# Two of four sums of weight tiles made by adding transfers; turned signs; the head's tokens in pairs of tiles

## The chip, the cores and the metric

The kernel runs on one core of one Trainium2 chip. The metric is the device time of one execution in microseconds; lower is better. TensorE multiplies matrices, VectorE and ScalarE work on tiles element by element, GpSimd does small vector work and can issue transfers, and SyncE (SP) issues nearly all loads. A transfer moves data between the chip's memory and SBUF through 16 DMA engines shared by all queues.

## The reference, cut to what matters

One decoder layer, float32, 256 tokens of 2048 features: a half-step SwiGLU, a mixer (latent attention and a gated recurrence), cross-attention to 256 memory tokens, and a second half-step SwiGLU. The change touches the two SwiGLUs (FFN 1 and 2), which hold most of the products:

```python
def swiglu(h, w_gate, w_up, w_down):          # w_gate, w_up: 2048 x 5504; w_down: 5504 x 2048
    return (jax.nn.silu(h @ w_gate) * (h @ w_up)) @ w_down

h = rmsnorm(x, ffn1_norm[l])
x = x + 0.5 * swiglu(h, ffn1_w_gate[l], ffn1_w_up[l], ffn1_w_down[l])
...
h = rmsnorm(x, ffn2_norm[l])
x = x + 0.5 * swiglu(h, ffn2_w_gate[l], ffn2_w_up[l], ffn2_w_down[l])
```

## The kernel before

Every float32 product is made as three matmuls in a faster float format: each operand is split into a high part (ScalarE, `w_hi`, `hT_hi`) and the rest (VectorE, `w_lo`, `hT_lo`), and TensorE does hi·hi, lo·hi and hi·lo. A tile is 128 x 512 weights (256 KB); the tokens are two tiles of 128.

Weights stream through a ring `raw` of RAW = 6 slots of four tiles (1 MB). SP fills slot c (semaphore `raw_loaded`, one for each place in the ring), ScalarE makes `w_hi` (a ring of three), VectorE `w_lo` (in place of the raw weights), TensorE uses it and counts `slot_used` twice for a slot. SP may load slot c when slot c - 6 is used up. All engines run their own instruction list in written order and meet only at semaphores, so nothing reorders itself.

Both FFNs begin with one plain pair of blocks (gate and up, four slots each). The head is that pair in FFN 1: slots 0 to 3 also need the turned tokens `xT` (16 tiles, tile k by semaphore `xT_in`), which ScalarE and VectorE split (`x_turned`). Everything after it is done in 28 "duos": pairs of 512-wide blocks, gate and up for the up-projections, two neighbouring column blocks for the down-projection. Two duos, the last up-pair of each FFN, are 384 wide. In a duo, three units (four in the first half's down-projections) each cover two tiles of depth in both blocks of weights with the seven products of a Strassen-Winograd scheme in place of eight, and plain slots cover the rest. A unit takes two slots: `raws[n]` holds its four weight tiles, the slot after it the four sums of them that the seven products need. VectorE made these sums (`combine`, L1249, L1251, L1253), after which ScalarE (`hi_made`, L798) and VectorE (`lo_parts`, L1261) split them. A duo of three units runs in TensorE as unit, plain, unit, plain, unit, plain (first block), then three plain slots (second block). A unit is 21 matmuls: `small` (P1), `acc` (A12), for the first unit of a duo then `tr` (P7), `small` (P6), `acc`, `acc`, `acc`; for later units one product of the raw slot comes before P7. P7 and P6 are the first that read the made slot.

`combine` before the change:

```python
dve.wait_ge(loaded[c % RAW], landed(c))
dve.wait_ge(slot_used, 2 * (c + 1 - RAW + 1))
v.tensor_tensor(made[:, 0:2, :], b[:, 1:4:2, :], b[:, 0:2, :], ALU.subtract).then_inc(ev("combined"), 1)
dve.wait_ge(ev("combined"), 2 * n + 1)
done(v.tensor_tensor(made[:, 2, :], b[:, 3, :], made[:, 0, :], ALU.subtract))
done.wait()
v.tensor_tensor(made[:, 3, :], b[:, 2, :], made[:, 2, :], ALU.subtract).then_inc(ev("combined"), 1)
```

Of the kernel before, what the change touches and what calls it, by code (L numbers as in the profile page):

```python
# [20 lines left out]
ALU = mybir.AluOpType  # L21
# [3 lines left out]
P = 128  # L25
NW = 512
# [101 lines left out]
def layer(nc, a, out):  # L128
# [18 lines left out]
    with ctx:  # L147
# [121 lines left out]
        loaded = [sem(f"raw_loaded{s}") for s in range(RAW)]  # L269
        hi_done = sem("hi_done")  # L270
# [10 lines left out]
        xT_in = [sem(f"xT_in{k}") for k in range(4 + 3)]  # L281
# [113 lines left out]
        for duo in DUOS:  # L395
            for r in duo.raws:
                fetches[r], fetches[r + 1] = 2 if duo.up else 1, 0
        M = slots["mix"]

        def landed(c):  # L400

            return 16 * sum(fetches[c % RAW:c + 1:RAW])

# [57 lines left out]

        @block.sync
        def _(sp):
# [6 lines left out]

            def rows_of(w, k0, tiles, cols):
                return w[k0 * P:(k0 + tiles) * P, cols].rearrange("(k p) n -> p k n", p=P)

            def load_duos(f):

                wg, wu, wd = (a[f"ffn{f}_w_{n}"][0] for n in ("gate", "up", "down"))
                for m in range(FIRST[f], LAST[f] + 1):
# [3 lines left out]
                    def load_unit(c, k):  # L481
# [43 lines left out]
            def load_first():  # L525
# [69 lines left out]
        def _(pool):  # L595
# [47 lines left out]
            done.wait()  # L643
            norm("x1")
            norm("mem")
# [40 lines left out]
            norm("x4")  # L686


        @block.scalar
        def _(act):  # L690
# [3 lines left out]
            def hi(c, rep, tiles, width):  # L694

                c += rep
                for i, (k0, k1) in enumerate(halves(tiles)):
                    if c == 1 and i == 0:
# [184 lines left out]
            def first_slots(s):  # L883

                for k in range(4):
# [5 lines left out]
                    else:  # L891
                        act.wait_ge(xT_in[3 + s], 16)
                        x_turned(4 * s + k)
                if s == 0:
                    act.wait_ge(first_hi, 4)
                    act.sem_inc(hi_done, 2)
                else:
                    hi(s, 0, 4, NW)
# [281 lines left out]
        def _(dve):  # L1180
# [4 lines left out]
            def lo(c, rep, tiles, width):  # L1185

                c += rep
                for i, (k0, k1) in enumerate(halves(tiles)):
                    dve.wait_ge(hi_done, 2 * c + i + 1)
# [38 lines left out]
            def token_sums(s1, rest, src):  # L1228

                done(v.tensor_tensor(s1, src[:, 0, P:SEQ], src[:, 1, P:SEQ], ALU.add))  # L1230
# [4 lines left out]
                v.tensor_tensor(rest[2], src[:, 1, 0:P], rest[0], ALU.subtract).then_inc(ev("sums_made"), 1)  # L1235
# [8 lines left out]
            def combine(c, n, width):  # L1244
# [63 lines left out]
            def take_parts(m):  # L1308
# [1095 lines left out]
```

## Time and profile before

| | |
|---|---|
| median of 3 runs | 1889.87 us (1889.83 to 1889.91) |
| profiled execution, its own time | 1891.52 us |
| its span, first to last instruction | 1889.6 us |
| PE busy | 1877.6 us, 99% |
| PEld (weight loads, beside PE) | 1576.3 us, 83% |
| VectorE (DVE) busy | 1550.7 us, 82% |
| ScalarE (ACT) busy | 1077.2 us, 57% |
| GpSimd (POOL) busy | 96.6 us, 5% |
| DMA | 362.55 MB, 57% of the 16 engines' time |
| granted TensorE clock | 1.00 throughout |

Busy time is the union of an engine's instructions; a matmul's modelled duration (0.39 us for 512 columns) overlaps the next one's. The busy share of an engine is an average over stages; what an engine waited for, and where, is read in the waits and the timeline.

### The profile page before, as it was taken

To read this page: it belongs to the slowest core of one execution; us is meant where nothing else is said; L and a number is where in the kernel's file an instruction comes from. 1 tells how busy PE (TensorE), PEld (TensorE's weight loads), DVE (VectorE), ACT (ScalarE), POOL (GpSimd) and SP (SyncE) were. 2 spreads that over 40 slices of the span, in tenths; PEclk is the share of its full clock that TensorE was granted. 3 is DMA by queue.
4 is the path that set the end of the run, shared out by engine and by line. 5 is a ranking of instruction groups with operands and counts; after the bars stand their busy time and mean duration, and the time that the engine had idled before them with its cause. 6 is when DMAs were issued, how large, how long until landed. Compare 5 with 4: busy or idle time off the path is not lost.

```text
span 1889.6 us, 23072 instructions
## 1 busy us (share of the span) xinstructions
PE 1877.6 (99%) x8836; PEld 1576.3 (83%) x8836; DVE 1550.7 (82%) x1955; ACT 1077.2 (57%) x1437; POOL 96.6 (5%) x98
## 2 busy tenths in 40 slices
PE   8999999999999999999999999999999999999999
PEld 7888888888889888988888888888888888888987
DVE  6999998888999877655666774689999978899986
ACT  6665555546556547545475655566565554555553
POOL 0000000000000001312250000000000000000000
PEclk9999999999999999999999999999999999999999
DMA  9655565655556674555443654456656665655654
GB/s 328 231 182 192 200 207 200 223 188 195 196 174 209 219 237 154 170 170 179 141 156 105 207 181 153 156 178 200 200 179 203 220 216 174 212 190 185 199 191 171
DMA packets 176862, 362.55 MB, mean 192 GB/s; under 512 B 8048, under 2 KB 19312, under 8 KB 176112
## 3 DMA queue, kind: packets, MB, share of 16 engines
q1 hardware_dynamic: 176464, 360.89, 57.2%
q8 instruction: 70, 1.15, 0.2%
q14 instruction: 40, 0.33, 0.1%
q10 hardware_dynamic: 288, 0.19, 0.0%
HBM read 358.95 MB, written 2.10 MB: 191 GB/s over the span
## 4 chain that ended last, share of the span: by engine, by line
PE 96%; DVE 1%; ACT 1%; DMA 1%; POOL 1%; issue 0%; SPq 0%; DVEq 0%; ACTq 0%; POOLq 0%
PE acc L1889 19%; PE acc L1887 19%; PE acc L1888 19%; PE acc L1876 8%; PE acc L1878 8%; PE acc L1877 8%; PE small L1887 2%; PE small L1889 2%; PE small L1888 2%; PE small L2088 2%; PE tr L1845 1%; PE tr L1889 1%; PE tr L1887 1%; PE tr L1888 1%; PE tr L1903 1%; DMA w_raw<-in_ffn_w_gate 0%
## 5 line engine op out<-in xcount | busy, mean ns | idle before, releaser
L1261 DVE TENSOR_TENSOR w_lo<-w_raw,w_hi 128x1024 fp32r<-128x1024 f32 (+2 forms) x720 | 724.7, 1060 | 66.3 <-ACT w_hi L704 46.7
L704 ACT ACTIVATE w_hi<-w_raw 128x1024 fp32r<-128x1024 f32 (+4 forms) x552 | 513.2, 963 | 167.3 <-PE acc L1889 123.3
L1887 PE MATMUL acc<-w_hi,hT_hi 128*128 128x512 f32 (+1 forms) x920 | 354.9, 386 | 0.0
L1889 PE MATMUL acc<-w_lo,hT_hi 128*128 128x512 f32 (+1 forms) x920 | 353.3, 384 | 0.0
L1888 PE MATMUL acc<-w_hi,hT_lo 128*128 128x512 f32 (+1 forms) x920 | 352.9, 384 | 0.0
L1190 DVE TENSOR_TENSOR w_lo<-w_raw,w_hi 128x1024 fp32r<-128x1024 f32 (+1 forms) x184 | 217.9, 1225 | 60.2 <-ACT w_hi L704 58.8
L798 ACT ACTIVATE w_hi<-w_raw 128x1024 fp32r<-128x1024 f32 (+1 forms) x176 | 182.3, 1044 | 114.0 <-DVE w_raw L1249 59.8
L1887 PE MATMUL acc<-w_hi,actT_hi 128*128 128x512 f32 x548 | 213.9, 390 | 0.0
L1889 PE MATMUL acc<-w_lo,actT_hi 128*128 128x512 f32 x548 | 213.3, 389 | 0.0
L1888 PE MATMUL acc<-w_hi,actT_lo 128*128 128x512 f32 x548 | 213.2, 389 | 0.0
L1889 PEld LDWEIGHTS acc<-w_lo,hT_hi 128*128 128x128 f32 x920 | 172.7, 188 | 32.7
L1887 PEld LDWEIGHTS acc<-w_hi,hT_hi 128*128 128x128 f32 x920 | 172.7, 188 | 32.2 <-DVE stage L1318 0.2
L1888 PEld LDWEIGHTS acc<-w_hi,hT_lo 128*128 128x128 f32 x920 | 172.8, 188 | 31.8
L791 ACT ACTIVATE w_hi<-w_raw 128x512 fp32r<-128x512 f32 (+3 forms) x176 | 142.7, 829 | 94.4 <-PE acc L1889 93.5
L1876 PE MATMUL acc<-w_hi,hT_hi 128*128 128x512 f32 (+1 forms) x480 | 186.7, 389 | 4.5 <-DVE w_lo L1190 3.7
L1878 PE MATMUL acc<-w_lo,hT_hi 128*128 128x512 f32 (+1 forms) x480 | 184.5, 384 | 0.0
L1877 PE MATMUL acc<-w_hi,hT_lo 128*128 128x512 f32 (+1 forms) x480 | 184.2, 384 | 0.0
L1889 PEld LDWEIGHTS acc<-w_lo,actT_hi 128*128 128x128 f32 x548 | 102.9, 188 | 21.5
L1888 PEld LDWEIGHTS acc<-w_hi,actT_lo 128*128 128x128 f32 x548 | 102.9, 188 | 21.3
L1887 PEld LDWEIGHTS acc<-w_hi,actT_hi 128*128 128x128 f32 x548 | 102.9, 188 | 21.2
L1876 PEld LDWEIGHTS acc<-w_hi,hT_hi 128*128 128x128 f32 x480 | 90.2, 188 | 22.2 <-issue 4.5
L1249 DVE TENSOR_TENSOR w_raw<-w_raw 128x1024 f32<-128x1024 f32 (+1 forms) x88 | 105.4, 1198 | 0.0
(306 smaller groups left out, 2547.9 us busy)
## 6 DMA issues: line engine op xcount, KB each, us to landing
w_raw<-in_ffn_w_down SPq DMA_DIRECT2D x68, 1024.0 KB, 5.2
w_raw<-in_w_in SPq DMA_DIRECT2D x36, 1024.0 KB, 5.0
w_raw<-in_ffn_w_gate SPq DMA_DIRECT2D x38, 768.0 KB, 4.3
w_raw<-in_ffn_w_up SPq DMA_DIRECT2D x38, 768.0 KB, 4.4
w_raw<-in_ffn_w_gate SPq DMA_DIRECT2D x56, 512.0 KB, 3.9
w_raw<-in_ffn_w_up SPq DMA_DIRECT2D x54, 512.0 KB, 4.8
w_raw<-in_ffn_w_up SPq DMA_DIRECT2D x26, 1024.0 KB, 5.9
w_raw<-in_ffn_w_gate SPq DMA_DIRECT2D x24, 1024.0 KB, 5.1
```

What stands on the lines that cost most here:

```text
L704: nc.scalar.activation(piece(w_hi, c % SPLIT, k0, k1, width), piece(raw, c % RAW, k0, k1, width), ACT.Copy).then_inc(hi_done, 1)
L791: nc.scalar.activation(piece(w_hi, c % SPLIT, k0, k1, width), piece(raw, c % RAW, k0, k1, width), ACT.Copy).then_inc(hi_done, 1)
L798: nc.scalar.activation(piece(w_hi, c % SPLIT, k0, k1, width), piece(raw, c % RAW, k0, k1, width), ACT.Copy).then_inc(hi_done, 1)
L1190: v.tensor_tensor(piece(w_lo, c % RAW, k0, k1, width), piece(raw, c % RAW, k0, k1, width), piece(w_hi, c % SPLIT, k0, k1, width).bitcast(F ...
L1249: v.tensor_tensor(made[:, 0:2, :], b[:, 1:4:2, :], b[:, 0:2, :], ALU.subtract).then_inc(ev("combined"), 1)
L1261: v.tensor_tensor(piece(w_lo, c % RAW, k0, k1, width), piece(raw, c % RAW, k0, k1, width), piece(w_hi, c % SPLIT, k0, k1, width).bitcast(F ...
L1876: mm(dst, xh, wh, start=first and kk == 0, stop=False)
L1877: mm(dst, xl, wh, start=False, stop=False)
L1878: ins = mm(dst, xh, wl, start=False, stop=last and kk == tiles - 1)
L1887: mm(dst, lhs_hi, wh, start=first, stop=False)
L1888: mm(dst, lhs_lo, wh, start=False, stop=False)
L1889: return mm(dst, lhs_hi, wl, start=False, stop=last)
```

## The change

It does four things.

1. SP loads, right behind the first slot of a unit, two tiles of the right block (`right_rows`) into the first half of the made slot. GpSimd, once these have landed, issues two transfers that add in flight: the unit's first left tile onto the first of them, and the first right tile onto the second (`add_weights`, semaphore `weights_added`).
2. VectorE's `combine` waits for these and makes only the other two sums, by one-tile additions.
3. The scheme's signs are turned to suit, since transfers can add and not subtract: in the sums of activations (`token_sums`) and in two of the additions of `take_parts`.
4. In the head, token tiles 4 to 15 come in six transfers of two tiles in place of three of four; SP's waits in between are on other semaphores; ScalarE and VectorE split two token tiles, then half a weight slot, in turn, and TensorE waits for token tiles two at a time (`later_piece`).

```diff
+        def summed(c):
+            return 32 * sum(e == c or e < c and e % RAW == c % RAW for d in DUOS for e in [r + 1 for r in d.raws])
...
                             sp.dma_start(dst, rows_of(wd, f0 + k, 2, slice(2 * d.block * NW, 2 * (d.block + 1) * NW))).then_inc(loaded[c % RAW], 16)
+                        sp.wait_ge(slot_used, 2 * (c + 1 - RAW + 1))
+                        made = raw[:, (c + 1) % RAW, :].rearrange("p (k n) -> p k n", k=4)
+                        sp.dma_start(made[:, 0:2, 0:d.width], right_rows(m, k, 2)).then_inc(loaded[(c + 1) % RAW], 16)
...
-                x_tiles(4, 4, xT_in[4])
+                x_tiles(4, 2, xT_in[4])
                 sp.wait_ge(first_in[1], 16)
                 for b, done in enumerate((first_in[4], loaded[1])):
+                    if b:
+                        x_tiles(6, 2, xT_in[5])
...
-                for s in range(2, 4):
-                    sp.wait_ge(xT_in[2 + s], 16)
-                    x_tiles(4 * s, 4, xT_in[3 + s])
+                for s, landed_ in ((2, first_in[3]), (3, loaded[1])):
+                    sp.wait_ge(landed_, 16)
+                    x_tiles(4 * s, 2, xT_in[2 + 2 * s])
                     load(s, 0, rows_of(wg, 4 * s, 4, slice(0, NW)), 4, NW)
+                    x_tiles(4 * s + 2, 2, xT_in[3 + 2 * s])
...
+            def add_weights(f):
+                for m in range(FIRST[f], LAST[f] + 1):
+                    d = DUOS[m]
+                    for n, c in enumerate(d.raws):
+                        c += 1
+                        made = raw[:, c % RAW, :].rearrange("p (k n) -> p k n", k=4)
+                        pool.wait_ge(loaded[c % RAW], landed(c))
+                        for i, rows in enumerate((left_rows, right_rows)):
+                            nc.gpsimd.dma_start(made[:, i:i + 1, 0:d.width], rows(m, d.units[n], 1), accum_op=ALU.add).then_inc(added[c % RAW], 16)
+
             norm("x1")
+            add_weights(1)
             norm("mem")
...
             norm("x4")
+            add_weights(2)
...
                 for i, (k0, k1) in enumerate(MADE_PARTS):
-                    act.wait_ge(ev("combined"), 2 * n + i + 1)
+                    if i == 0:
+                        act.wait_ge(added[c % RAW], summed(c))
+                    else:
+                        act.wait_ge(ev("combined"), 2 * n + 2)
...
-                done(v.tensor_tensor(s1, src[:, 0, P:SEQ], src[:, 1, P:SEQ], ALU.add))
+                done(v.tensor_tensor(s1, src[:, 0, P:SEQ], src[:, 1, P:SEQ], ALU.subtract))
...
-                v.tensor_tensor(rest[2], src[:, 1, 0:P], rest[0], ALU.subtract).then_inc(ev("sums_made"), 1)
+                v.tensor_tensor(rest[2], src[:, 1, 0:P], rest[0], ALU.add).then_inc(ev("sums_made"), 1)
...
                 dve.wait_ge(loaded[c % RAW], landed(c))
-                dve.wait_ge(slot_used, 2 * (c + 1 - RAW + 1))
-                v.tensor_tensor(made[:, 0:2, :], b[:, 1:4:2, :], b[:, 0:2, :], ALU.subtract).then_inc(ev("combined"), 1)
+                dve.wait_ge(added[(c + 1) % RAW], summed(c + 1))
+                v.tensor_tensor(made[:, 2, :], made[:, 1, :], b[:, 0, :], ALU.add).then_inc(ev("combined"), 1)
                 dve.wait_ge(ev("combined"), 2 * n + 1)
-                done(v.tensor_tensor(made[:, 2, :], b[:, 3, :], made[:, 0, :], ALU.subtract))
-                done.wait()
-                v.tensor_tensor(made[:, 3, :], b[:, 2, :], made[:, 2, :], ALU.subtract).then_inc(ev("combined"), 1)
+                v.tensor_tensor(made[:, 3, :], made[:, 2, :], b[:, 2, :], ALU.add).then_inc(ev("combined"), 1)
...
-                done(v.tensor_tensor(nat[:, 0, 0:w], p5, nat[:, 0, 0:w], ALU.add))
+                done(v.tensor_tensor(nat[:, 0, 0:w], p5, nat[:, 0, 0:w], ALU.subtract))
                 done.wait()
-                v.tensor_tensor(nat[:, 1, 0:w], p5, gate[:, 1, 0:w], ALU.add).then_inc(ev("parts_taken"), 1)
+                v.tensor_tensor(nat[:, 1, 0:w], p5, gate[:, 1, 0:w], ALU.subtract).then_inc(ev("parts_taken"), 1)
```

VectorE's list at the second unit of the first duo, before; L1249, L1251 and L1253 are the sums, L1261 low parts of weights, L1270 that of activations:

```order
42 L1249 TENSOR_TENSOR w_raw<-w_raw 128x1024 [waits slot_used,raw_loaded5]
43 L1251 TENSOR_TENSOR w_raw<-w_raw 128x512 [waits combined]
44 L1253 TENSOR_TENSOR w_raw<-w_raw 128x512 [waits dve_done]
45 L1261 TENSOR_TENSOR w_lo<-w_raw,w_hi 128x512 [waits hi_done]
46 L1261 TENSOR_TENSOR w_lo<-w_raw,w_hi 128x1024 [waits hi_done,combined]
47 L1270 TENSOR_TENSOR actT_lo<-tr,actT_hi 128x512 [waits turn_hi]
```

The same place in the changed kernel (its L1300 and L1302 are the sums, L1310 and L1319 the low parts):

```order
47 L1300 TENSOR_TENSOR w_raw<-w_raw 128x512 [waits weights_added0,raw_loaded5]
48 L1302 TENSOR_TENSOR w_raw<-w_raw 128x512 [waits combined]
49 L1310 TENSOR_TENSOR w_lo<-w_raw,w_hi 128x512 [waits hi_done]
50 L1310 TENSOR_TENSOR w_lo<-w_raw,w_hi 128x1024 [waits hi_done,combined]
51 L1319 TENSOR_TENSOR actT_lo<-tr,actT_hi 128x512 [waits turn_hi]
```

The two-tile sum is gone, and the first instruction left waits for the adding transfers with everything else behind it.

GpSimd's list in the changed kernel after the norm of the first tokens (before, the norm of the memory stood here next):

```order
8 L632 TENSOR_SCALAR rsq<-sums 128x2 [waits sums_x1,pool_done]
9 L634 TENSOR_TENSOR rsq<-rsq,minus_half 128x2 [waits pool_done]
10 L683 DMA w_raw<-in_ffn_w_gate 128x512 [waits raw_loaded3]
11 L683 DMA w_raw<-in_ffn_w_up 128x512
12 L683 DMA w_raw<-in_ffn_w_gate 128x512 [waits raw_loaded0]
```

Two adding transfers for each unit follow on each other in the order of the units.

SP's list in the head, before; `xT_raw` are the turned tokens:

```order
8 L528 DMA xT_raw<-in_x_turned 128x1024
9 L538 DMA w_raw<-in_ffn_w_gate 128x2x512 [waits first_slot_in1]
10 L538 DMA w_raw<-in_ffn_w_gate 128x2x512
11 L528 DMA xT_raw<-in_x_turned 128x1024 [waits xT_in4]
12 L469 DMA w_raw<-in_ffn_w_gate 128x4x512
13 L528 DMA xT_raw<-in_x_turned 128x1024 [waits xT_in5]
14 L469 DMA w_raw<-in_ffn_w_gate 128x4x512
```

And in the changed kernel:

```order
8 L555 DMA xT_raw<-in_x_turned 128x512
9 L567 DMA w_raw<-in_ffn_w_gate 128x2x512 [waits first_slot_in1]
10 L555 DMA xT_raw<-in_x_turned 128x512
11 L567 DMA w_raw<-in_ffn_w_gate 128x2x512
12 L555 DMA xT_raw<-in_x_turned 128x512 [waits first_slot_in3]
13 L495 DMA w_raw<-in_ffn_w_gate 128x4x512
14 L555 DMA xT_raw<-in_x_turned 128x512
15 L555 DMA xT_raw<-in_x_turned 128x512 [waits raw_loaded1]
16 L495 DMA w_raw<-in_ffn_w_gate 128x4x512
17 L555 DMA xT_raw<-in_x_turned 128x512
```

The tokens stand in smaller pieces around the weights, and SP waits for weights that land earlier, no longer for the tokens themselves.

## Rows read from the trace of the kernel before

**Rows 1.** The page: span, busy time and share of the two busiest engines.
```profile
span 1889.6 us, 23072 instructions
...
PE 1877.6 (99%) x8836; PEld 1576.3 (83%) x8836; DVE 1550.7 (82%) x1955; ACT 1077.2 (57%) x1437; POOL 96.6 (5%) x98
```

**Rows 2.** Waits of PE: total us, times, longest.
```profile
PE acc L1876 <- DVE w_lo L1190: 3.7, 2, 1.9
```

**Rows 3.** Timeline of PE, head: start, us, engine, what [idle before].
```profile
14.14 0.47 PE L1876 MATMUL acc<-w_hi,hT_hi 128*128 128x512 f32 x1 [1.78 <-DVE w_lo L1190]
...
21.80 0.47 PE L1876 MATMUL acc<-w_hi,hT_hi 128*128 128x512 f32 x1 [1.94 <-DVE w_lo L1190]
```

**Rows 4.** Timeline of PE, first unit of the third duo.
```profile
140.32 0.39 PE L1888 MATMUL acc<-w_hi,hT_lo 128*128 128x512 f32 x1
140.55 0.39 PE L1889 MATMUL acc<-w_lo,hT_hi 128*128 128x512 f32 x1
141.44 0.50 PE L1887 MATMUL tr<-w_hi,hS_hi 128*128 128x512 f32 x1 [0.50 <-DVE w_lo L1261]
...
142.58 0.50 PE L1887 MATMUL small<-w_hi,hS_hi 128*128 128x512 f32 x1 [0.17 <-DVE w_lo L1261]
```

**Rows 5.** One line's instructions: ns min/median/max, first and last start.
```profile
L1249 DVE TENSOR_TENSOR w_raw<-w_raw x88: 946/1216/1221, 49.4 to 1848.5; 128x1024 f32<-128x1024 f32 x82, 128x768 f32<-128x768 f32 x6
```

**Rows 6.** Windows: busy time (count) of each engine, clock, DMA share, GB/s.
```profile
core 0: us, PE busy (x) PEld busy (x) DVE busy (x) ACT busy (x) POOL busy (x), PEclk, DMA share, GB/s
...
16.00:19.00 3.00, 3.00 (x15) 2.47 (x14) 1.68 (x4) 1.71 (x4) 0.00 (x0) 1.00 0.55 148
...
30.00:45.00 15.00, 15.00 (x67) 12.40 (x67) 7.79 (x17) 10.88 (x16) 0.34 (x2) 1.00 1.01 381
...
145.00:300.00 155.00, 155.00 (x700) 128.10 (x699) 148.13 (x178) 89.09 (x110) 0.00 (x0) 1.00 0.61 205
```

**Rows 7.** Units' first products (P1) in three duos: durations, first and last start.
```profile
L1887 PE MATMUL small<-w_hi,hT_hi x3: 389/389/389, 183.2 to 203.2; 128*128 128x512 f32 x3
...
L1887 PE MATMUL small<-w_hi,hT_hi x3: 389/389/389, 394.2 to 413.3; 128*128 128x512 f32 x3
...
L1887 PE MATMUL small<-w_hi,hT_hi x3: 333/334/334, 563.0 to 578.5; 128*128 128x384 f32 x3
```

**Rows 8.** Timeline of SP: second half of the third unit's load.
```profile
187.88 0.47 SPq L487 DMA_DIRECT2D w_raw<-in_ffn_w_up  x1
```

**Rows 9.** The page's DMA issues: count, KB each, median us to landing.
```profile
w_raw<-in_ffn_w_down SPq DMA_DIRECT2D x68, 1024.0 KB, 5.2
...
w_raw<-in_ffn_w_gate SPq DMA_DIRECT2D x56, 512.0 KB, 3.9
```

**Rows 10.** DMA issues at 187.88, and at 33.09.
```profile
w_raw<-in_ffn_w_up SPq DMA_DIRECT2D x1, 512.0 KB, 4.9
...
w_raw<-in_ffn_w_up SPq DMA_DIRECT2D x1, 512.0 KB, 11.0
```

**Rows 11.** Timeline of DVE before the third unit of the fourth duo.
```profile
199.18 1.21 DVE L1249 TENSOR_TENSOR w_raw<-w_raw 128x1024 f32<-128x1024 f32 x1
...
201.76 5.22 DVE L1261 TENSOR_TENSOR w_lo<-w_raw,w_hi 128x512 fp32r<-128x512 f32 x5
```

**Rows 12.** Timeline of ACT, head: tokens, then high parts of slot 1.
```profile
10.08 1.71 ACT L901 ACTIVATE hT_hi<-xT_raw,gains 128x256 fp32r<-128x256 f32 x4 [0.64 <-DMA xT_raw<-in_x_turned]
11.70 2.03 ACT L704 ACTIVATE w_hi<-w_raw 128x1024 fp32r<-128x1024 f32 x2
```

**Rows 13.** The chain that ended last, head: start, us, what.
```profile
10.46 8.86 DMA w_raw<-in_ffn_w_gate
```

**Rows 14.** Timeline, the first unit of all: sums, low part, first product.
```profile
49.37 1.22 DVE L1249 TENSOR_TENSOR w_raw<-w_raw 128x1024 f32<-128x1024 f32 x1
...
51.95 4.09 DVE L1261 TENSOR_TENSOR w_lo<-w_raw,w_hi 128x512 fp32r<-128x512 f32 x4
...
54.52 0.39 PE L1887 MATMUL small<-w_hi,hT_hi 128*128 128x512 f32 x1
```

More of the change, by code:

```diff
@@ L269, in layer @@
         loaded = [sem(f"raw_loaded{s}") for s in range(RAW)]
+        added = [sem(f"weights_added{s}") for s in range(RAW)]
         hi_done = sem("hi_done")
@@ L280, in layer @@
         gains_in, ident_in, const_in, x_in, mem_in = sem("gains_in"), sem("ident_in"), sem("const_in"), sem("x_in"), sem("mem_in")
-        xT_in = [sem(f"xT_in{k}") for k in range(4 + 3)]
+        xT_in = [sem(f"xT_in{k}") for k in range(4 + 6)]
         first_in = [sem(f"first_slot_in{k}") for k in range(4 + 1)]
@@ L396, in layer @@
             for r in duo.raws:
-                fetches[r], fetches[r + 1] = 2 if duo.up else 1, 0
+                fetches[r], fetches[r + 1] = 2 if duo.up else 1, 1
         M = slots["mix"]
@@ L459, in layer, with rows_of, columns_of, right_rows @@
         block = ctx.enter_context(nc.Block())
+        def rows_of(w, k0, tiles, cols):
+            return w[k0 * P:(k0 + tiles) * P, cols].rearrange("(k p) n -> p k n", p=P)
+        def columns_of(m, side):
+            d = DUOS[m]
+            f0 = HALVES[d.half][0]
+            n0 = (f0 + 4 * d.block) * P if d.up else (2 * d.block + side) * NW
+            w = a[f"ffn{d.f}_w_{('gate', 'up')[side] if d.up else 'down'}"][0]
+            return w, 0 if d.up else f0, slice(n0, n0 + d.width)
+        def right_rows(m, k, tiles):
+            w, k0, cols_ = columns_of(m, 1)
+            return rows_of(w, k0 + k, tiles, cols_)
+        def left_rows(m, k, tiles):
+            w, k0, cols_ = columns_of(m, 0)
+            return rows_of(w, k0 + k, tiles, cols_)
         @block.sync
@@ L469, in load @@
                 sp.dma_start(dst, src).then_inc(loaded[c % RAW], 16)
-            def rows_of(w, k0, tiles, cols):
-                return w[k0 * P:(k0 + tiles) * P, cols].rearrange("(k p) n -> p k n", p=P)
             def load_duos(f):
@@ L692, in _, with hi @@
             flat_stage = stage[:].rearrange("p a b -> p (a b)")
-            def hi(c, rep, tiles, width):
+            def hi(c, rep, tiles, width, part=None):
                 c += rep
                 for i, (k0, k1) in enumerate(halves(tiles)):
+                    if part not in (None, i):
+                        continue
                     if c == 1 and i == 0:
@@ L891, in first_slots @@
                     else:
-                        act.wait_ge(xT_in[3 + s], 16)
+                        if k % 2 == 0:
+                            act.wait_ge(xT_in[2 + 2 * s + k // 2], 16)
                         x_turned(4 * s + k)
+                        if k % 2:
+                            hi(s, 0, 4, NW, part=k // 2)
                 if s == 0:
@@ L896, in first_slots @@
                     act.sem_inc(hi_done, 2)
-                else:
-                    hi(s, 0, 4, NW)
             def x_turned(k):
@@ L1183, in _, with lo @@
             flat_stage = stage[:].rearrange("p a b -> p (a b)")
-            def lo(c, rep, tiles, width):
+            def lo(c, rep, tiles, width, part=None):
                 c += rep
                 for i, (k0, k1) in enumerate(halves(tiles)):
+                    if part not in (None, i):
+                        continue
                     dve.wait_ge(hi_done, 2 * c + i + 1)
@@ L1414, in first_slots @@
                                         w_hi[:, 0, k * NW:(k + 1) * NW].bitcast(F32), ALU.subtract).then_inc(first_lo, 1)
+                    elif k % 2:
+                        lo(s, 0, 4, NW, part=k // 2)
                 if s == 0:
@@ L1417, in first_slots @@
                     dve.sem_inc(lo_done, 2)
-                else:
-                    lo(s, 0, 4, NW)
             def x_turned(k):
@@ L1854, in of, with later_piece, wait @@
                 return lambda m, t: src[:, t, col0 + m * P:col0 + (m + 1) * P]
+            def later_piece(s):
+                def wait(kk):
+                    if kk % 2 == 0:
+                        pe.wait_ge(x_lo, 4 * s + kk + 2)
+                return wait
             def first_piece(kk):
@@ L2050, in first_pair @@
                         if f == 1 and b == 0:
-                            pe.wait_ge(x_lo, 4 * s + 1 if s == 0 else 4 * s + 4)
-                            pieces = first_piece if s == 0 else None
+                            pieces = first_piece if s == 0 else later_piece(s)
                         slot(c + 4 * b + s, 0, B0 + b, hT_hi, hT_lo, 4 * s, 4, NW, s == 0, s == 3, pieces=pieces)
```

1 line of the change is left out of this document (added).

## The prediction, made blind

> **What bounds the kernel now.** Read the page first: TensorE has matmuls in flight for 1877.6 of 1889.6 us, VectorE works 82% of the span [rows 1]. The waits of PE say how little TensorE gives away: 3.7 us for w_lo at L1190, and nothing else of size inside the two FFNs [rows 2]. The timeline shows where: idle for 1.78 us before 14.14 and 1.94 us before 21.80 [rows 3]. Between these places a 128x512 matmul starts every 0.23 us (140.32 to 140.55) [rows 4]. The one loss inside an FFN stands in the same rows: the first unit of the third duo starts its third product (three matmuls) at 141.44, 0.89 us after the matmul before in place of 0.23, and the fourth at 142.58, 1.14 us later in place of 0.69. That is 0.66 + 0.45 = 1.1 us, some 1.2 with the restart behind it. So VectorE is busy but almost nowhere late, and the instructions taken from it can give back only what is idle: 3.7 us in the head and 1.2 us here. Everything else the change does can only cost.
>
> **What VectorE loses.** Before, a unit's sums are a subtraction of two tiles, 1.2 us, 88 times [rows 5], and two of one tile; from 199.18 to 201.76 the three take 2.6 us [rows 11]. The two-tile one goes, 1.4 us stay. That frees 88 x 1.2 = 106 us of VectorE. Of this, TensorE sees one place: at 141.44 the chain is subtraction, sums of activations, split, low part, all on VectorE and ScalarE. 1.2 us earlier there takes away nearly all of the 1.2 us: I take **-1.1 us**. In all other units TensorE waits for nothing of theirs, so the value is nothing.
>
> **What the transfers gain in work.** A unit's two slots held one 1 MB load. Now SP also loads two tiles (512 KB) into the second slot, and GpSimd adds two tiles of 256 KB to it. A 512-wide duo of three units is 3 x 21 + 20 x 6 = 183 matmuls, 42 us at 0.23, in which 3 + 5 = 8 MB came; now 11 MB will. By the windows the share of the DMA engines was 0.61 at 205 GB/s; with full queues they carried 381 GB/s at a share of 1.01 [rows 6]. 11 MB of 1024 x 1024 bytes in 42 us is 275 GB/s, 72% of 381. If an added byte costs as two (read the old sum, read the tile), it is 12.5 MB, 312 GB/s, 82%. So the mean rate fits in both cases; what counts is the delay of each chain.
>
> **The chain of a made slot and its time limit.** Take the unit that starts at 203.2. Its second slot comes free when the first unit of this duo ends: 183.2 + 21 x 0.23 = 188.0 [rows 7]. SP issues the two halves of the first slot's load at about that time, the last at 187.88, taking 0.47 [rows 8]; the new load follows at 188.4. Alone, 512 KB take 3.9 us [rows 9], giving 192.3; behind the 1 MB, whose last half lands 4.9 us after its issue, at 192.8 [rows 10], the added 0.52 MB at 381 GB/s give 194.2. I take the later one. Then GpSimd sees the semaphore and issues two adds, and both must land before VectorE can go on. VectorE now waits for them *ahead* of the first sum; queued behind this are the low parts of the unit's own first slot, which TensorE needs from 203.2 on. Before, the sums started at 199.18 and the low parts at 201.76; the second of these, after 0.69 + 1.2 us at 203.6, serves the product at 203.9, with only 0.3 us to spare [rows 11]. With 1.4 in place of 2.6 us the sums may start at 200.6. The adds have 200.6 - 194.2 = **6.4 us** (8.3 at best).
>
> No row of this case has a GpSimd transfer or an adding one. Bounds: no less than one plain 512 KB load, 3.9 us; no more than two adds one after the other, each with the cost of a plain 1 MB load, 5.2 us [rows 9], 10.4 us. I take the two adds overlapping, each byte as two: 1 MB in all, 5.2 us, and 0.4 us for the second issue (SP's is 0.47 [rows 8]; GpSimd's own price is unknown): **5.6 us**, nearer to the lower end since SP's two halves overlap in flight, the second landing 4.9 us after its own issue. That is 0.8 us inside the limit.
>
> The Trainium skill (Collectives: The Full Stack, Stop ④ and the part on why ReduceScatter is half of AllGather) says that an adding transfer is slow not by its addition but since it reads two sources on one ring. No trace here shows it. By it the two adds are 1 MB of reading, as taken above; without it they would be a plain 512 KB, 3.9 + 0.4 = 4.3 us, and the result would be about 2 us lower than forecast, since the terms below would vanish.
>
> Other windows are shorter. In the duos whose first and third unit start at 394.2 and 413.3 (four of these), the distance is 19.1 instead of 20.0 us: limit 5.5, late by 0.1 to 0.2, together +0.5 us. In the 384-wide duos (two), it is 15.5 us: less 3.6 for the unit, about 2.1 for sums and low parts in VectorE and 5.7 for the loads (6.2 above, for a quarter more bytes) leaves 4.1 us, against perhaps 4.9 for adds of 192 KB: +0.8 each, **+1.6 us** [rows 7]. A delay of TensorE by d also moves all later limits by d, so lateness counts once per overlapping window, not per unit.
>
> **The head.** Tokens now come in pairs of tiles, the first pair issued at 4.00 where four were. ScalarE turned four tiles, 1.71 us, before the first high part at 11.70 [rows 12]. With two the high part can start 0.4 to 1.0 us earlier (its weights must land), and so can TensorE at 14.14. The next stop, 21.80, ends with a load issued at 10.46 that took 8.86 us [rows 13]; between 16 and 19 the DMA share was only 0.55 [rows 6], since SP held back the next tokens until the last had come. Now SP waits for an earlier semaphore and there are 256 KB less ahead: 0.7 us at 381 GB/s, and up to 0.45 x 3 = 1.35 us more where the idle share is filled. TensorE is thus ahead by 0.7 to 2.1 us, and by no more than the 3.7 us that it idled.
> What is late next: the first unit, at 54.52. Its sums started at 49.37 [rows 14]. The new load of its second slot queues behind one that landed at 33.09 + 11.0 = 44.1 [rows 10], while the DMA share is 1.01: 0.52 MB / 381 = 1.4 us more, less 0 to 1.3 us by the idle share now filled: 44.2 to 45.5. With 5.6 us for the adds the sums start at 49.8 to 51.1. From their start to the end of the last low part that this unit needs, 51.95 + 4.09 = 56.04, were 6.7 us; now 5.5. That part serves the fourth product, 9 x 0.23 = 2.1 us after the unit's start, so TensorE can start the unit 3.4 us after the sums, at 53.2 to 54.5. Of the head's lead -1.3 to 0 us stay: I take **-0.6 us**.
>
> Removing the waits costs no instruction; turned signs replace an operation by another of the same shape: nothing. GpSimd's norm of the memory (rsq_mem) now stands behind all adds of the first FFN, and is first used in cross-attention, after the whole mixer: nothing.
>
> Sum: -1.1 + 0.5 + 1.6 - 0.6 = +0.4 us. On the profiled execution's span of 1889.6 us that is 1890.0; its own time was 1891.52, the median of the three runs 1889.87. Forecast of the median: **1890 us**.
>
> **Rivals.**
> (a) The adds are late (slower). From 6.4 us on each duo pays the excess about once: 28 duos. At 7.5 us it is 28 x 1.1 = 31 us, some 1920 us; at the upper end of 10.4 us, 28 x 4 = 112 us and more in four-unit duos: 2000 us. For it: an unmeasured issue cost and a DMA queue shared with SP's loads of the next slots; against it: the mean rate fits. Chance 0.30.
> (b) The adds are quick (4 us) and the head keeps its lead: -2.1 - 1.2 = -3.3 us, 1886.6, at the very best -3.7 - 1.2, 1885.0. The first needs the first unit's sums to start at 49, so adds within about 4 us, and is not yet 0.2%. With mechanisms not seen: chance 0.13.
> (c) The DMA engines become the bound: each added byte would have to cost as five plain ones (9.5 + 1.5 x 5 = 17 MB, at 381 GB/s = 47 us against 42), then 28 x 4 us: 2000. Against it: no row hints at this. Chance 0.05.
> (d) GpSimd cannot write its transfers' descriptors while VectorE holds a shared port; VectorE is 95% busy between 145 and 300 (148.13 of 155 us) [rows 6], so issue could slip by one instruction of 1.22 us each time, 2.4 us for two adds: 5.6 + 2.4 = 8.0, 1.6 us late in 28 duos, 1935 us. The Trainium skill (SBUF — State Buffer, the "DVE blocks DMA" trap) names this for VectorE's two-port modes only, which it does not give to tensor_tensor. No run here shows it. Chance 0.07.
>
> **How the numbers follow.** A measurement of this kernel tells 0.2%, 3.8 us, from no change. The forecast with its variants from 1886.1 to 1893.6: 0.45. Slower: (a), (c) and (d), 0.42. Faster: (b), 0.13. The range takes in the bounds of the head and the adds to about 7.8 us (1930): 1885.5 to 1935; beyond it lie about 2 in 10. The likeliest case alone: 1886 to 1893.
>
> **What would show it.** In the profile after: VectorE busy about 106 us less; no two-tile w_raw row; the two head stops at under 1 us together; an interval of 0.23 us where 141.44 stood; a start of the first unit near 54. PE's waits tell (a): waits for w_lo of the first-slot low part, at the third unit first, with VectorE's releaser a transfer into w_raw. In (c) the DMA share would be near 1 across the FFNs. I am wrong if adds take over 6.4 us from the landing of the plain load.

## The result, and the profile after

| | before | after |
|---|---|---|
| median of 4 runs each, same chip | 1889.89 us | 2069.96 us (2060.72 to 2075.47) |
| profiled execution, span | 1889.6 us | 2065.6 us (its own time 2067.38) |

The ratio is 1.0944, 95% interval 1.0923 to 1.0964: the kernel is slower by 180 us, far outside the range of 1885.5 to 1935. What follows is read from the profile after.

The page, lines that answer to [rows 1], with the adding transfers' queue (q0, GpSimd's: packets, MB, share of 16 engines):

```profile
span 2065.6 us, 23254 instructions
...
PE 1947.8 (94%) x8836; PEld 1604.2 (78%) x8836; DVE 1451.3 (70%) x1867; ACT 1068.4 (52%) x1437; POOL 245.6 (12%) x274
...
DMA packets 226575, 453.28 MB, mean 219 GB/s; under 512 B 12320, under 2 KB 26656, under 8 KB 225824
...
q0 software_dynamic: 25344, 45.36, 13.0%
...
PE 63%; DMA 27%; DVE 5%; issue 2%; POOL 2%; SPq 1%; ACT 1%; DVEq 0%; POOLq 0%; ACTq 0%
```

VectorE has given up 99 us, as meant. The span is 176.0 us longer, and TensorE is busy for 70.2 us of that, with the same 8836 matmuls: so there are two losses, 106 us in which it stands still, and 70 us in which it is busy for longer at the same work. Each needs its own cause. The last line is the one to stop at: over a quarter of the chain that ended last is now transfers.

The waits by total time (us, times, longest) say who stands in line:

```profile
POOL w_raw L683 <- DMA w_raw<-in_ffn_w_up: 840.9, 59, 26.7
...
DVE w_raw L1300 <- DMA w_raw<-in_ffn_w_up: 186.8, 57, 9.1
...
DVE w_raw L1300 <- DMA w_raw<-in_ffn_w_down: 116.2, 25, 10.2
...
PE small L1943 <- DVE w_lo L1310: 106.0, 40, 5.6
```

GpSimd's 840.9 us cost nothing in themselves (it has nothing else to do); VectorE's 303 us at L1300, the first sum, are waits for the adds; TensorE's 106 us are the low part queued behind that sum. Nearly all of it is at the third unit of a duo. One such unit, the third of the fourth duo, as the chain that ended last shows it (start, us, what); [rows 7, 8, 11] are the same unit before:

```profile
198.89 0.24 PE acc L1945
199.13 0.02 issue
199.15 0.37 SPq L510
199.51 0.04 issue
199.56 0.56 SPq L510
200.12 0.04 issue
200.17 7.33 DMA w_raw<-in_ffn_w_up
207.50 0.28 issue
207.78 0.54 POOL w_raw L683
208.32 8.30 DMA w_raw<-in_ffn_w_up
216.62 0.03 issue
...
216.71 0.70 DVE w_raw L1300
...
218.04 0.69 DVE w_lo L1310
218.74 0.04 issue
218.78 0.79 PE small L1943
```

Read down: the slot comes free (199.13), SP issues the raw slot's halves and then the plain load (L517), which takes 7.33 us; GpSimd issues the first add 0.28 us later and the second 0.54 us after that; the second lands 8.30 us after its issue; two sums and a low part, and TensorE starts. The unit starts 23.9 us after the duo's first one (194.85 to 218.78); before, 20.0 [rows 7].

The second loss shows in the windows around that start (length, then busy time of each engine, granted clock, DMA share, GB/s):

```profile
210.00:218.70 8.70, 5.48 (x25) 4.20 (x23) 3.67 (x7) 2.35 (x3) 0.00 (x0) 0.97 1.01 309
218.78:221.50 2.72, 2.72 (x6) 2.10 (x7) 2.72 (x3) 2.72 (x4) 0.00 (x0) 0.50 0.42 152
221.50:230.00 8.50, 8.50 (x39) 7.03 (x38) 8.43 (x11) 3.26 (x5) 0.71 (x2) 0.99 0.54 185
```

After standing still for 3.30 us TensorE gets a clock of 0.50, the lower of its two levels (1.2 GHz), for 2.7 us: 6 matmuls where 12 fit. The page counts that as busy. The 0.97 in the window before says that the clock had fallen already within the stop.

The transfers' times to landing (count, KB, median us):

```profile
w_raw<-in_ffn_w_up SPq DMA_DIRECT2D x108, 512.0 KB, 5.4
...
w_raw<-in_ffn_w_up SPq DMA_DIRECT2D x26, 1024.0 KB, 8.5
...
w_raw<-in_ffn_w_down POOLq DMA_DIRECT2D x56, 256.0 KB, 7.1
w_raw<-in_ffn_w_gate POOLq DMA_DIRECT2D x54, 256.0 KB, 6.3
w_raw<-in_ffn_w_up POOLq DMA_DIRECT2D x54, 256.0 KB, 7.7
```

Over all 88 units, unit by unit from the issues: both adds have landed 8.12 us (median) after the first one's issue; for the 18 third units of 512-wide up duos 9.08 us, behind a plain load of 6.61 us.

The head, answering to [rows 3, 14]: its second stop is gone, and the first unit starts 2.5 us earlier.

```profile
12.98 0.50 PE L1932 MATMUL acc<-w_hi,hT_hi 128*128 128x512 f32 x1 [0.41 <-DVE w_lo L1241]
...
52.01 0.47 PE L1943 MATMUL small<-w_hi,hT_hi 128*128 128x512 f32 x1 [0.62 <-DVE w_lo L1310]
```

### The profile page after: what moved, and what is told of

Its sections match the earlier page's. It is cut to its first block, busy times and chain, and to the rows that moved or that the text cites. A ratio compares the mean times of both kernels' runs of the same rounds, so it can differ in the third digit from the quotient of the medians.

```text
span 2065.6 us, 23254 instructions
## 1 busy us (share of the span) xinstructions
PE 1947.8 (94%) x8836; PEld 1604.2 (78%) x8836; DVE 1451.3 (70%) x1867; ACT 1068.4 (52%) x1437; POOL 245.6 (12%) x274
## 3 DMA queue, kind: packets, MB, share of 16 engines
q0 software_dynamic: 25344, 45.36, 13.0%
## 4 chain that ended last, share of the span: by engine, by line
PE 63%; DMA 27%; DVE 5%; issue 2%; POOL 2%; SPq 1%; ACT 1%; DVEq 0%; POOLq 0%; ACTq 0%
DMA w_raw<-in_ffn_w_up 18%; PE acc L1943 10%; PE acc L1944 10%; PE acc L1945 10%; DMA w_raw<-in_ffn_w_down 8%; PE acc L1932 7%; PE acc L1934 7%; PE acc L1933 7%; DVE w_lo L1310 3%; PE small L1943 2%; PE small L2143 1%; PE small L1945 1%; PE small L1944 1%; PE tr L1894 1%; DVE w_raw L1300 1%
## 5 line engine op out<-in xcount | busy, mean ns | idle before, releaser
L1310 DVE TENSOR_TENSOR w_lo<-w_raw,w_hi 128x1024 fp32r<-128x1024 f32 (+2 forms) x720 | 722.4, 1059 | 48.4 <-ACT w_hi L749 41.3
L749 ACT ACTIVATE w_hi<-w_raw 128x1024 fp32r<-128x1024 f32 (+4 forms) x552 | 506.6, 960 | 148.2 <-PE acc L1945 106.7
L1943 PE MATMUL acc<-w_hi,hT_hi 128*128 128x512 f32 (+1 forms) x920 | 361.0, 392 | 2.0 <-DVE w_lo L1310 1.4
L1300 DVE TENSOR_TENSOR w_raw<-w_raw 128x512 f32<-128x512 f32 (+1 forms) x88 | 60.1, 683 | 303.1 <-DMA w_raw<-in_ffn_w_up 186.8
L1943 PEld LDWEIGHTS acc<-w_hi,hT_hi 128*128 128x128 f32 x920 | 174.4, 190 | 43.7 <-DVE w_lo L1310 10.8
L1932 PE MATMUL acc<-w_hi,hT_hi 128*128 128x512 f32 (+1 forms) x480 | 186.7, 389 | 0.4 <-DVE w_lo L1241 0.4
L683 POOL DMA_DIRECT2D w_raw<-in_ffn_w_gate x60 | 52.3, 872 | 841.1 <-DMA w_raw<-in_ffn_w_up 840.9
```

What stands on the lines that cost most here:

```text
L749: nc.scalar.activation(piece(w_hi, c % SPLIT, k0, k1, width), piece(raw, c % RAW, k0, k1, width), ACT.Copy).then_inc(hi_done, 1)
L1300: v.tensor_tensor(made[:, 2, :], made[:, 1, :], b[:, 0, :], ALU.add).then_inc(ev("combined"), 1)
L1310: v.tensor_tensor(piece(w_lo, c % RAW, k0, k1, width), piece(raw, c % RAW, k0, k1, width), piece(w_hi, c % SPLIT, k0, k1, width).bitcast(F ...
L1932: mm(dst, xh, wh, start=first and kk == 0, stop=False)
L1943: mm(dst, lhs_hi, wh, start=first, stop=False)
```

## The experiments

Line numbers below are those of each kernel. The kernel before ran beside each on the same chip (medians 1890.4, 1891.5 and 1891.1 us in the three sets; differences below are against these).

**1. The head alone, and with the signs.** Kernel A is the kernel before with the edits of the head (tokens in pairs, `hi` and `lo` by halves, `later_piece`). Kernel B adds the turned signs and leaves the transfers out:

```diff
-                fetches[r], fetches[r + 1] = 2 if duo.up else 1, 1
+                fetches[r], fetches[r + 1] = 2 if duo.up else 1, 1 if in_flight(duo, duo.raws.index(r)) else 0
...
+                else:
+                    dve.wait_ge(slot_used, 2 * (c + 1 - RAW + 1))
+                    v.tensor_tensor(made[:, 0:2, :], b[:, 1:4:2, :], b[:, 0:2, :], ALU.add).then_inc(ev("combined"), 1)
```

with `in_flight` always False; the second piece stands in `combine`, and SP's load, GpSimd's adds and ScalarE's wait for them are skipped likewise.

> The kernel before with the head's edits alone (tokens in pairs of tiles, first FFN block split half a slot at a time). In the changed kernel the two stops of the head shrank from 3.7 to 0.4 us, and its first unit began at 52.0 in place of 54.5. If the head's part is good by itself, and nothing behind it is late, its time is that of before less 2.5 to 3.3 us, some 1886.8. Rival: the lead is lost again at the first unit, whose sums begin only when its loads have landed (49.4 before); then it is 1889 to 1890.

> The changed kernel without its transfers for the sums: no second load into the made slot, no adding transfer, all four sums by VectorE (one instruction of two tiles, two of one), but with the turned signs and the new head. The signs exchange an operation for another of the same shape: the theory is the same time as the kernel with the head's edits alone, within 1 us. Rival: the turned signs lengthen a chain that TensorE waits for (more than 1 us apart, and a wait of PE that the head's kernel does not have).

A: 1888.47 us (11 runs), ratio 0.9987 (0.9978 to 0.9996). B: 1888.37 us (11 runs), 0.9989 (0.9980 to 0.9998). The head is worth 1.9 us, most of its lead, and the signs nothing. The expected 1886.8 was 1.7 us too low; both of its outcomes lie close, and the median is between them. So the 180 us are in the sums' transfers and in the waits that come with them.

**2. The head of before, with the transfers.**

> The changed kernel with the head of before. The loss of 180 us is all in the adding transfers by the theory, so it is that of the changed kernel plus the 2 to 3 us of the head: 2070 to 2074. Rival: the head's new order of loads (SP's queue) is what makes the first FFN late; then the time is lower than the changed kernel's by more than 5 us.

2066.55 us (2061.17 to 2071.89, 4 runs), ratio 1.0929 (1.0908 to 1.0951). The whole loss again; the 2070 to 2074 expected were a little too high, and the head's 2 us don't show among runs 10 us apart.

**3. Adds for one unit of each duo only.** Three kernels, 28 units each, of 88:

```diff
-            return False
+            return n == 0        # and n == 1, n == 2
```

> The changed kernel with adding transfers only for the first unit of each duo (28 of 88 units); the other sums are made by VectorE. Theory, the chain is late only where its time is short: in the changed kernel TensorE hardly waits at a duo's first or second unit (0 to 1 us) and 3.3 us at the third. Then this kernel loses at most 0 to 1 us a duo, and lies between 1886 and 1900, with fewer than 5 us of PE's waits for w_lo in the FFNs. Rival, the adding transfers cost by their number (traffic, contention in the DMA engines): a third of the loss of 180 us, some 1945 to 1950.

> The changed kernel with adding transfers only for the third unit of each duo (28 of 88 units). Theory, the chain is late where its time is short: these units have 6.4 us by the prediction and the two adds land 8.1 us after the first is issued, so nearly all stalls come back: 2.5 to 3.5 us of idle TensorE in 28 duos, 70 to 100 us, and with the slowed matmuls behind each stall 110 to 170 us: 2000 to 2060. Rival, cost by number: the same as with the adds at the first unit only, where it was +28 us (some 1916).

> The changed kernel with adding transfers only for the second unit of each duo (28 of 88). In the changed kernel the second unit's two adds have landed 11.7 us after the issue of the right load (third: 16.5). Theory, every unit has its own time limit: little of the loss is here, 1888 to 1905. Since the first units alone cost 28 and the third alone 100 us, and all together 180, the rest of 50 us is then in the adds of one duo hindering each other (third units' adds land 16.5 us after the right load's issue with all adds in flight, 14.2 with theirs alone). Rival: the second units' adds hold the 50 us themselves, 1925 to 1950.

First units: 1916.45 us (ratio 1.0137, 1.0123 to 1.0152), +26 us. Second units: 1902.93 us (1.0064, 1.0050 to 1.0078), +12 us. Third units: 1991.56 us (1.0531, 1.0509 to 1.0552), +100 us. Same count, same bytes (391.40 MB each), a factor of eight: the cost does not go by number. Only the second units came out as expected. TensorE's waits, third, first and second units:

```profile
PE small L1960 <- DVE w_lo L1327: 62.9, 29, 5.6
```
```profile
PE small L1960 <- DVE w_lo L1327: 12.1, 10, 5.4
```
```profile
PE small L1960 <- DVE w_lo L1327: 2.7, 5, 1.3
```

In the second units' kernel the waits are too few for its +12 us. Its page and one of its short stops say where they are:

```profile
PE 1887.8 (99%) x8836; PEld 1574.3 (83%) x8836; DVE 1518.7 (80%) x1927; ACT 1070.2 (56%) x1437; POOL 144.2 (8%) x154
...
276.39 0.50 PE L1960 MATMUL small<-w_hi,actT_hi 128*128 128x512 f32 x1 [0.82 <-DVE w_lo L1327]
276.72 0.40 PE L1961 MATMUL small<-w_hi,actT_lo 128*128 128x512 f32 x1
```

TensorE is busy for 10.2 us more than before [rows 1], and the granted clock of this run never falls to 0.50: behind a wait even this short the next matmuls start 0.33 us and once 0.56 us apart in place of 0.23, and that counts as busy.

The first units held a miss: I expected under 5 us of waits and at most 1900, and two stops carry most of it, 5.4 and 4.6 us at the first unit behind each 384-wide duo (604 and 1806 us): the 384-wide matmuls ahead of it leave the chain less time (argued from their length, not tested). The rest of the +26 us is busy time again (1891.1 us). The third units fell below the 2000 to 2060 expected. The three sum to 138 us of the 180; the rest is what the units do to each other (and the fourth units, in none of the three). Only the third units suffer from the others: alone, their two adds have landed 14.5 us after the plain load's issue, with all in flight 16.6; for the first units the two figures are 12.6 and 12.4 us, for the second 11.8 and 11.8.

**4. The same two transfers without the addition.** GpSimd loads the same tiles to the same place, so the two sums are not made and the output leaves them out:

```diff
-    nc.gpsimd.dma_start(made[:, i:i + 1, 0:d.width], rows(m, d.units[n], 1), accum_op=ALU.add).then_inc(...)
+    nc.gpsimd.dma_start(made[:, i:i + 1, 0:d.width], rows(m, d.units[n], 1)).then_inc(...)
```

> The changed kernel with GpSimd's two transfers of each unit as plain loads of the same tiles instead of adding ones (so the two sums are not made, and the output leaves them out). Theory 1, the time is in the issue by GpSimd and the way through its queue: plain loads then also land 7 to 8 us after the first issue, and the loss is nearly the changed kernel's, 2040 to 2070. Theory 2, the time is in the adding (two reads and a write for each byte): then they land in 4 to 5 us, inside the limit of 6.4, and the time is 1890 to 1920.

1928.60 us (1921.36 to 1930.48, 4 runs), ratio 1.0189 (1.0168 to 1.0209): +37 us where the adding ones cost 180. Both have landed 5.83 us after the first issue (median of 88), not 8.12. So neither theory holds alone: two plain transfers from GpSimd already use up most of the limit, and some units fail in it; the addition's 2.3 us put nearly all third units behind it. The queue's own line, beside that of the changed kernel above:

```profile
q0 software_dynamic: 13888, 45.36, 6.9%
...
w_raw<-in_ffn_w_down POOLq DMA_DIRECT2D x56, 256.0 KB, 4.9
w_raw<-in_ffn_w_gate POOLq DMA_DIRECT2D x54, 256.0 KB, 4.4
w_raw<-in_ffn_w_up POOLq DMA_DIRECT2D x54, 256.0 KB, 5.2
```

6.9% of 1927.0 us is 133 us of the 16 engines; 13.0% of 2065.6 is 269 us, for the same bytes: an added byte costs 2.0 times a plain one in the engines.

**5. The same bytes, all loaded by SP.** VectorE waits for both loads and then makes all four sums itself (against kernel B):

```diff
+    sp.dma_start(made[:, 0:2, 0:d.width], right_rows(m, k, 2)).then_inc(loaded[(c + 1) % RAW], 16)
+    sp.dma_start(made[:, 2:4, 0:d.width], left_rows(m, k, 2)).then_inc(loaded[(c + 1) % RAW], 16)
...
-    dve.wait_ge(slot_used, 2 * (c + 1 - RAW + 1))
+    dve.wait_ge(loaded[(c + 1) % RAW], landed(c + 1))
     v.tensor_tensor(made[:, 0:2, :], b[:, 1:4:2, :], b[:, 0:2, :], ALU.add).then_inc(ev("combined"), 1)
```

> The changed kernel without GpSimd's transfers: SP loads the same bytes, two right and two left tiles (512 KB each) into the made slot, VectorE waits for both and then makes all sums itself over them. Theory, traffic is not the bound: two queued plain loads land within 7 us of the first issue and the VectorE chain is 1.2 us longer, so single stalls under 1.5 us at the third units, 1890 to 1930. Rival, 11 MB a duo is too much for the DMA engines beside the matmuls: the same loss as the changed kernel, 2050 or more, with every load (w_down and w_up slots too) landing later by 2 us and more.

1889.02 us (10 runs), ratio 0.9986 (0.9976 to 0.9995), the same as without the loads.

```profile
PE 1879.1 (100%) x8836; PEld 1576.9 (84%) x8836; DVE 1551.4 (82%) x1955; ACT 1078.2 (57%) x1437; POOL 96.6 (5%) x98
...
q1 hardware_dynamic: 224768, 451.60, 70.9%
```

The page has 91 MB more than before, and TensorE is busy for 1879.1 of 1887.5 us. The bytes alone cost nothing: the mean rate fits, as predicted. The chain is short here since it has one step: the second load has landed 5.6 us (median) after its issue, 7.5 us at the worst kind of unit.

**6. Stalls without any added transfer.** The kernel before, whose third units' two-tile sum is done five times:

```diff
+                for _ in range(again):
+                    done(v.tensor_tensor(made[:, 0:2, :], b[:, 1:4:2, :], b[:, 0:2, :], ALU.subtract))
+                    done.wait()
...
-                            combine(d.raws[n], u0 + n, w)
+                            combine(d.raws[n], u0 + n, w, 4 if n == 2 else 0)
```

> The kernel before (no added traffic, no GpSimd transfer, old head); for the third unit of each duo VectorE does the two-tile sum five times instead of once, 4 x 1.22 = 4.9 us more ahead of the split. Question: are the slowed matmuls of the changed kernel (TensorE 70 us busier at the same count) due to the stalls or to the traffic. Theory, stalls: TensorE idles 3.5 to 4.6 us in 28 duos, 100 to 130 us, and is also busier by 40 to 80 us, granted clock below 1 behind each stall; 2030 to 2090. Rival, traffic: TensorE is idle as long, but its busy time stays at 1878 us and the clock at 1.00; 1990 to 2020.

2019.02 us (2018.14 to 2019.63, 4 runs), ratio 1.0673 (1.0657 to 1.0689). The waits of PE, the page's line, then three windows around the start at 79.91 and two around one at 449.59:

```profile
PE small L1890 <- DVE w_lo L1264: 77.0, 29, 4.3
```
```profile
PE 1927.1 (96%) x8836; PEld 1598.7 (79%) x8836; DVE 1685.3 (84%) x2067; ACT 1073.8 (53%) x1437; POOL 96.6 (5%) x98
```
```profile
76.00:79.90 3.90, 0.12 (x1) 0.00 (x0) 3.80 (x6) 1.67 (x2) 0.00 (x0) 0.97 1.05 420
79.90:83.00 3.10, 3.09 (x7) 2.45 (x8) 3.10 (x3) 2.86 (x4) 0.00 (x0) 0.50 0.85 322
83.00:90.00 7.00, 7.00 (x32) 5.75 (x31) 6.93 (x10) 3.13 (x4) 0.00 (x0) 1.00 0.48 152
447.00:449.50 2.50, 1.42 (x7) 0.84 (x5) 2.43 (x5) 1.59 (x2) 0.00 (x0) 1.00 0.61 218
449.60:453.00 3.40, 3.24 (x13) 2.36 (x14) 3.40 (x4) 3.36 (x5) 0.00 (x0) 1.00 0.69 227
```

TensorE is 49.5 us busier than before [rows 1] with no byte more: the slowed matmuls come from its stalls, not from traffic. Matmul by matmul against the trace of before, 38 us of this lie in stretches with a granted clock of 0.50, 12 us elsewhere. Behind the stop that ends at 79.91 (4.17 us between two starts) the clock is 0.50 for about 3 us. Behind the one that ends at 449.59 (1.56 us) it is 1.00: 13 matmuls in 3.4 us. So a short stop costs itself and, in the 5 us behind it, 0.6 us; behind the 22 stops in the FFNs that the lower clock follows it is 41 us together, 1.9 us each. The time lay 11 us below the expected 2030, since TensorE stood still for 77 us, not 100: the five sums were 4.9 us longer and TensorE stood for 3.1 to 4.5 us in most duos, for 1.3 to 2.1 in six.

**7. One add a unit instead of two, and nobody in VectorE waits for it.** SP loads right tile k (256 KB), GpSimd adds left tile k; VectorE makes the other three sums one tile at a time, from the raw slot; only ScalarE's `hi_made` waits for the transfer:

```diff
-                dve.wait_ge(added[(c + 1) % RAW], summed(c + 1))
+                dve.wait_ge(slot_used, 2 * (c + 1 - RAW + 1))
+                v.tensor_tensor(made[:, 1, :], b[:, 3, :], b[:, 1, :], ALU.add).then_inc(ev("combined"), 1)
```

> The changed kernel with one adding transfer a unit in place of two, for all 88 units: right tile k (256 KB, SP) plus left tile k (256 KB, added by GpSimd); the other three sums are made by VectorE, one tile each, and do not wait for the transfer; only the high part of the made slot does. Theory: the chain is shorter by the second add (about 3 us) and by half of the right load, and its limit longer, since VectorE's three sums (2 us) run beside it; one adding transfer then lands 9 to 13 us after the right load's issue, in time, and the time is 1887 to 1892. Rival: adding transfers cost by being there (contention, GpSimd's issue): half of the loss, 1950 or more.

1891.29 us (1889.22 to 1897.72, 11 runs), ratio 1.0009 (1.0000 to 1.0018), with 88 adding transfers (22.68 MB in queue 0) in place. They land 4.88 us after their issue and 9.8 us after the plain load's (medians). TensorE's waits are at the level of the head's kernel:

```profile
PE acc L1935 <- DVE w_lo L1242: 1.1, 2, 0.6
```

and the adding transfers' landings (count, KB, median us):

```profile
w_raw<-in_ffn_w_gate POOLq DMA_DIRECT2D x54, 256.0 KB, 4.9
w_raw<-in_ffn_w_down POOLq DMA_DIRECT2D x28, 256.0 KB, 6.1
```

So 88 adding transfers as such cost little; what costs is a chain longer than its limit. They aren't free either: by the ratios (1.0009 against 0.9987) this kernel is 0.2%, some 4 us, slower than kernel A, whose head it shares, though VectorE works 1510.4 us here, 41 us less. Its trace is of its fastest run and doesn't show where the others lose this. And the run changes two things, one add fewer (with half of the plain load ahead) and nothing in VectorE waiting for it; no run tells which of them was needed.

## Why the prediction was wrong

**What held.** TensorE was the bound, VectorE's relief was worth nothing that a time shows, the signs cost nothing, the mean rate fits (experiment 5), an added byte costs as two, and the place and order of the new wait were right: VectorE's first sum waits for the adds, the low part behind it is late, the third unit stands. Rival (a) named this mechanism, at a chance of 0.30; the likeliest case, adds inside the limit, was the wrong one.

**The step that failed** is the chain of the made slot: "I take the two adds overlapping, each byte as two: 1 MB in all, 5.2 us, and 0.4 us for the second issue: 5.6 us ... 0.8 us inside the limit." Two terms were mis-sized:
- *The adds.* 0.28 us from landing to issue, 0.54 us between the issues, and 9.08 us from the first issue to the last landing at the third units; 8.12 in the median of all. Predicted 5.6. The bytes were counted rightly, but a duration that SP's loads have for 1 MB was given to another queue: even plain, GpSimd's two 256 KB take 5.83 us where SP's 512 KB take 3.9 [rows 9], and adding brings them to 8.12. Both bounds of the prediction held, 3.9 and 10.4 us; the point taken between them rested on no row of such a transfer, and the upper one lay nearer.
- *The plain load ahead.* Its issue was put right: 0.95 us after SP's first issue for the unit (187.47 in the trace of before, to 188.4), 1.02 us in the chain above. Predicted to land 5.8 us later, it takes 6.61 us at the third units. With adds at the third units alone (experiment 3) it takes 5.56 us there, so the excess comes from the other units' adds. In the unit shown, the second unit's adds are in flight from 196.11 to 203.25, beside this load (200.17 to 207.50). The third unit's own adds (207.78 to 216.62) then run beside three loads of plain slots issued at 205.77, 208.24 and 211.43, and from 210 to 218.7 the DMA share is 1.01: 9.08 us, where with the third units' adds alone it is 8.24. The second units' plain load takes 3.7 us. The *mean* share of 72 to 82% was right (0.80 from 150 to 700 us) and said nothing of this.

Put right, the sum by the prediction's own limit of 6.4 us is: 6.61 - 5.8 = 0.8 us for the load, 0.28 + 9.08 - 6.4 = 3.0 us for the adds, 3.8 us late in all. The unit shown has lost 3.9 (23.9 against 20.0), and 28 times 3.8 is 106 us, the 106 us that TensorE waits. The rule "once per overlapping window" was good; that the product fits so closely is partly luck, since single waits are as long as 5.6 us and the duos of the down-projections have other limits.

**The term that was missing** is what a stall costs behind it. 106 us of idle would give 1996; the time is 2070, since TensorE is also busy for 70 us more. Compared matmul by matmul with the trace of before, 49 us of these (all three rounded) lie in the 26 stretches in which the granted clock is 0.50 (113 us in all); 12 us lie in the intervals of the stops themselves and 10 us between other matmuls, at clock 1.00. The second kind is what the second units' kernel of experiment 3 shows by itself. Behind the 26 stops that the lower clock follows, TensorE loses 2.0 us each in the next 5 us. Experiment 6 shows the same without the transfers. The trace of before did not show it: behind its two stops of 1.78 and 1.94 us [rows 3] the matmuls ran at full rate.

**The single terms.** The two-tile interval at 141.44: in the changed kernel the first products of that duo's first and second unit are 10.85 us apart (11.96 before), with no such gap. That is the 1.1 us, but TensorE comes to this unit 8 us late there, so it doesn't show the term by itself. In experiment 7, where TensorE isn't late and VectorE's sums are 0.5 us shorter (three of one tile), the interval of 0.89 us is down to 0.36, so the term was likely real, and drowned. The gap stayed in kernel A, whose sums are as before (0.5 and 0.2 us of waits for w_lo in the waits of PE). The 384-wide windows (+1.6) were no special case: late like the rest. The head: predicted -0.6, measured -1.9 us (experiment 1, without the transfers). In the changed kernel three steps of it were off and partly cancel: the first unit's plain load lands at 41.84, not at 44.2 to 45.5; its adds take 7.6 us, not 5.6; and the unit starts 2.2 us after its sums, not 3.4: at 52.01, not at 53.2 to 54.5.

**The rivals.** (a) was right in mechanism; its upper price of 2000 us counted the stalls alone and was too low by what they cost behind them. (c), DMA engines as the bound, fell: 451.60 MB in experiment 5 cost nothing, and an added byte costs the engines 2.0 plain ones, not five. But they have a part in the chain: with other units' adds in flight the third units' load lands later (6.61 against 5.56 us). (d), descriptors blocked by VectorE: the first add is issued 0.28 us after the landing (median of 88; the same for the 79 landings that find VectorE at work and for the 9 that find it idle), the second 0.54 us later. The Trainium skill (SBUF — State Buffer, the "DVE blocks DMA" trap) does not give this to tensor_tensor; the trace agrees. The Trainium skill (Collectives: The Full Stack, Stop ④ and the part on why ReduceScatter is half of AllGather) says that an adding transfer pays for two sources read; the trace agrees, with 269 us of the engines against 133 for the same 45.36 MB. But the adding ones are also cut into more packets, 25344 against 13888, and no run tells the two apart.

## What to carry to other kernels

A mean rate that fits says nothing about a chain of transfers that wait for each other: add up issue, landing, issue, landing at the moment of the duo when most other transfers are in flight, and compare it with the limit of the tightest unit, not of the typical one. Work taken off an engine that nobody waits for is worth nothing, and if it moves into a chain of transfers ahead of that engine's next instruction, everything queued behind is late with it. If a sum must come by transfer, let only its own reader wait, and give it one adding step: both together worked in experiment 7. A stall costs more than its length: count what the trace shows behind it.

The best kernels here are A, B and that of experiment 5, 1888.4 to 1889.0 us, 0.11 to 0.14% below the kernel before by their ratios: the tokens in pairs are what remains of the change.

## What the runs showed of the hardware that was not expected

- Two 256 KB transfers from GpSimd's queue: 5.83 us plain, 8.12 us adding, until both have landed; one adding alone 4.88 us. An adding one occupies GpSimd for 0.85 to 1.26 us, a plain one for 0.54 to 0.74 us. The adding ones are cut into 25344 packets where the plain ones have 13888.
- TensorE's clock behind its stops, in the head and the FFNs of all twelve traces, by the time between two matmul starts: of the 24 stops from 1.3 to 1.94 us none was followed by a granted clock of 0.50; of the 24 from 1.95 to 2.95 us 16 were (not the two stops of before, 2.17 and 2.32 us in the head, but experiment 6's of 2.30 us in the same place); above 3 us 78 of 79 were. The slowed stretch holds 5 to 11 matmuls 0.43 us apart in place of 0.23 where they are 512 wide. A long stall's price is its length and some 2 us.
- A stop costs more than its length at full clock too: 0.6 us in the 5 us behind one of 1.56 us (experiment 6).
